# Expert loop of a hybrid layer: the down product runs one block later, weights arrive in halves, one Silu table load

## The reference

```python
def hier_moe(h, ...):                 # 32 experts, each token goes to 2
    ...
    padded = ((counts + MOE_BLOCK - 1) // MOE_BLOCK) * MOE_BLOCK   # MOE_BLOCK = 128
    ...
    def expert_block(args):
        xb, e = args                  # 128 rows of one expert
        hid = jax.nn.silu(xb @ w_gate[e]) * (xb @ w_up[e])
        return hid @ w_down[e]
    ...
```

## Time and profile before

| | |
|---|---|
| median of 3 runs | 2628.35 us (2627.71 to 2632.11) |
| span of the profiled execution | 2631.2 us |
| PE busy | 2182.8 us, 83% |
| DVE busy | 1414.4 us, 54% |
| ACT busy | 1110.2 us, 42% |
| DMA moved | 458.84 MB, mean 174 GB/s |

### The profile page before, as it was taken

One profiled execution on the slowest core, in us unless ns is written; L12 is line 12 of the kernel. 1 busy time (PEld: TensorE's weight loads), 2 busy tenths in 40 slices (PEclk: granted clock), 3 DMA queues, 4 the chain that ended last, 5 costly groups with the idle time before them and its releaser, 6 DMA issues. The chain is left out here.

```text
span 2631.2 us, 29505 instructions
## 1 busy us (share of the span) xinstructions
PE 2182.8 (83%) x9771; PEld 1642.8 (62%) x9772; DVE 1414.4 (54%) x2372; ACT 1110.2 (42%) x1586; POOL 310.3 (12%) x380
## 2 busy tenths in 40 slices
PE   4999999868969687785999219999999999999950
PEld 4764444357447676675888107777777777777740
DVE  4832581044358567584444527466647847354548
ACT  6101111013227566574222017566648847454432
POOL 0002331025020110000000220000000000000022
PEclk9999999979869899898999559999999999999985
DMA  7023433173651431502443057477668967445649
GB/s 220 34 78 136 168 136 116 51 263 128 260 142 46 100 71 43 112 1 71 140 140 125 17 208 296 197 273 311 250 244 308 368 248 300 186 187 203 252 169 377
DMA packets 129203, 458.84 MB, mean 174 GB/s; under 512 B 26192, under 2 KB 42720, under 8 KB 114784
## 3 DMA queue, kind: packets, MB, share of 16 engines
q1 hardware_dynamic: 98512, 345.28, 37.6%
q0 software_dynamic: 19952, 69.51, 7.1%
q10 hardware_dynamic: 10656, 43.00, 4.0%
HBM read 342.09 MB, written 115.65 MB: 174 GB/s over the span
## 5 line engine op out<-in xcount | busy, mean ns | idle before, releaser
L1532 DVE TENSOR_TENSOR w_gate_lo<-w_gate_raw,w_gate_hi 128x2048 fp32r<-128x2048 f32 x64 | 146.3, 2287 | 180.0 <-ACT w_gate_hi L1487 180.0
L895 DVE CUSTOM_DVE_ANT_0 scores<-c_bank,alibi 128x512 f32<-128x512 f32 (+3 forms) x320 | 175.4, 607 | 109.1 <-PE c_bank L993 108.9
L488 PE MATMUL a_bank<-w_in_chunk,hT 128*128 128x512 f32 x512 | 222.1, 596 | 0.7 <-ACT hT L266 0.7
L488 PE MATMUL a_bank<-hT,w_in_chunk 128*128 128x512 f32 x512 | 220.6, 593 | 0.0
L300 ACT ACTIVATE proj_out<-a_bank 128x512 f32<-128x512 f32 x64 | 38.2, 597 | 398.1 <-PE a_bank L488 387.8
L488 PEld LDWEIGHTS a_bank<-w_in_chunk,hT 128*128 128x128 f32 x512 | 128.8, 252 | 92.6 <-issue 62.8
L1007 PE MATMUL c_bank<-v_head,map_T 128*128 128x128 f32 x1088 | 152.0, 288 | 41.6 <-ACT map_T L951 41.6
L1575 PE MATMUL m_bank<-w_gate_hi,rows_T_hi 128*128 128x512 f32 x392 | 155.0, 395 | 24.1 <-DVE rows_T_lo L1536 24.1
L1613 PE MATMUL m_bank<-w_down_hi,hidden_T_hi 128*128 128x512 f32 x392 | 161.2, 411 | 16.5 <-ACT hidden_T_hi L1509 16.5
L488 PEld LDWEIGHTS a_bank<-hT,w_in_chunk 128*128 128x128 f32 x512 | 97.1, 190 | 120.8 <-issue 120.7
L1007 PEld LDWEIGHTS c_bank<-v_head,map_T 128*128 128x128 f32 x1088 | 135.9, 198 | 57.2 <-ACT map_T L951 57.2
(11 more groups left out here) (370 smaller groups left out, 4429.1 us busy)
## 6 DMA issues: line engine op xcount, KB each, us to landing
w_gate_raw<-in_w_gate_dram SPq DMA_DIRECT2D x32, 2048.0 KB
w_up_raw<-in_w_up_dram SPq DMA_DIRECT2D x32, 2048.0 KB
w_down_raw<-in_w_down_dram SPq DMA_DIRECT2D x32, 2048.0 KB
rows_d<-rows_out ACTq DMA_DIRECT2D x50, 512.0 KB, 10.5
rows_d<-zero_rows POOLq DMA_DIRECT2D x34, 512.0 KB
x_tile<-in_x_dram SPq DMA_DIRECT2D x16, 512.0 KB
w_in_chunk<-in_w_in_dram POOLq DMA_DIRECT2D x4, 2048.0 KB, 19.1
qT_d<-xn_tile SPq DMA_DIRECT2D x32, 256.0 KB
```

Source lines behind the costliest of these rows:

```text
L488: last = pe.matmul(bank[4 + n % PB][:], lhsT, rhs, start=kt == 0, stop=kt == KT - 1)
L895: dve.tensor_tensor_reduce(S[:, s, m, c * BANK:c * BANK + w], bank[n % 4][:, 0:w], bias[:, h % 2, x0:x0 + w], 1.0, -BIG, ALU.add, ALU.max, ...
L1532: dve.tensor_tensor(wlo[w][:, s], raw[w][:, s], whi[w][:, s], ALU.subtract).then_inc(lo_done[w], 1)
```

## The change

The down product of a block is issued one block later: TensorE's loop body is now gate product of block j + 1, hidden transposes of j, up product of j + 1, all eight row transposes of j + 2, down product of j. The first gate and up products stand ahead of the loop, the last block's hidden transposes and down product behind it, and the loop has one turn less (`META_LATER`, one more step in `route`). Each weight is loaded in two halves with a semaphore each, and each half waits for its own half of high and low part only. ACT makes both halves of the output. ACT and DVE get new orders, and split the first rows ahead of the first weights. ACT names the Silu table once ahead of its work.

```diff
+META_LATER = NBLK + NE + 2
+META = NBLK + NE + 3
...
+                step(dve.tensor_scalar(bf[:, META_LATER:META], pend[:, NE - 1:NE], -1.0, None, ALU.add))
...
-        w_in = [sem(f"w_{n}_in") for n in ("gate", "up", "down")]
+        w_in = [[sem(f"w_{n}_in{i}") for i in range(2)] for n in ("gate", "up", "down")]
...
+            later = lambda eng: eng.value_load(meta[0:1, META_LATER:META_LATER + 1], min_val=MIN_BLK - 1, max_val=NBLK - 2)
...
-                        sp.wait_ge(hi_done[w], 2 * o + 2)
-                        sp.wait_ge(lo_done[w], 2 * o + 2)
-                        sp.dma_start(raw[w][:], a[name][0, bass.ds(e, 1)].rearrange("o (p k) n -> p (o k n)", k=k)).then_inc(w_in[w], 16)
+                        src = a[name][0, bass.ds(e, 1)].rearrange("o (p k) n -> p (o k n)", k=k)
+                        for i in range(2):
+                            sp.wait_ge(hi_done[w], 2 * o + 1 + i)
+                            sp.wait_ge(lo_done[w], 2 * o + 1 + i)
+                            sp.dma_start(raw[w][:, halves[i]], src[:, halves[i]]).then_inc(w_in[w][i], 16)
...
+                def out_half(h, b):
+                    act.wait_ge(d_done, 2 * b + h + 1)
+                    if h == 0:
+                        act.wait_ge(out_st, 16 * b + 16)
+                    act.activation(out[:, h * BANK:(h + 1) * BANK], DN[h][:], ACT.Copy).then_inc(d_used, 1)
...
+                act.preload_act_table(ACT.Silu)
                 rows_hi(0, 1)
                 rows_hi(1, 2)
+                for w in range(3):
+                    split_hi(w, 0, 0)
+                    split_hi(w, 0, 1)
+                first, second = place(act, 0), place(act, 1)
+                act.wait_ge(g_done, 1)
+                act.activation(sil[:], G[:], ACT.Silu).then_inc(silu_done, 1)
+                with where_below(nc, act, first, second):
+                    split_hi(0, second, 0)
+                    split_hi(0, second, 1)
+                rows_hi(0, 3)
+                rows_hi(1, 4)
+                with where_below(nc, act, first, second):
+                    act.wait_ge(u_done, 1)
+                    split_hi(1, second, 0)
+                    split_hi(1, second, 1)
+                with act.Fori(0, later(act)) as j:
+                    before, now, order = place(act, j), place(act, j + 1), place(act, j + 2)
+                    hidden_hi(j + 1)
+                    act.wait_ge(g_done, j + 2)
+                    act.wait_ge(hid_done, j + 1)
                     act.activation(sil[:], G[:], ACT.Silu).then_inc(silu_done, 1)
                     with where_below(nc, act, now, order):
+                        split_hi(0, order, 0)
+                        split_hi(0, order, 1)
+                    rows_hi(0, 2 * j + 5)
+                    rows_hi(1, 2 * j + 6)
                     with where_below(nc, act, now, order):
+                        act.wait_ge(u_done, j + 2)
+                        split_hi(1, order, 0)
+                    out_half(0, j)
                     with where_below(nc, act, now, order):
+                        split_hi(1, order, 1)
+                    out_half(1, j)
+                    store(j)
+                    with where_below(nc, act, before, now):
+                        split_hi(2, now, 0)
+                        split_hi(2, now, 1)
+                end = later(act)
+                hidden_hi(end + 1)
+                out_half(0, end)
+                out_half(1, end)
+                store(end)
...
+                with dve.Fori(0, later(dve)) as j:
+                    before, now, order = place(dve, j), place(dve, j + 1), place(dve, j + 2)
+                    hidden_lo(j + 2)
                     with where_below(nc, dve, now, order):
+                        split_lo(0, order, 0)
+                        split_lo(0, order, 1)
+                    hidden(j + 1)
+                    rows_lo(0, 2 * j + 5)
+                    rows_lo(1, 2 * j + 6)
                     with where_below(nc, dve, now, order):
+                        split_lo(1, order, 0)
+                        split_lo(1, order, 1)
+                    with where_below(nc, dve, before, now):
+                        split_lo(2, now, 0)
+                        split_lo(2, now, 1)
+                end = later(dve)
+                hidden_lo(end + 2)
...
+                with pe.Fori(0, later(pe)) as j:
+                    before, order = place(pe, j), place(pe, j + 1)
+                    pe.wait_ge(xh_done, 2 * j + 4)
+                    pe.wait_ge(xl_done, 2 * j + 4)
+                    pe.wait_ge(silu_done, j + 1)
+                    pe.wait_ge(hi_done[0], 2 * order + 4)
+                    pe.wait_ge(lo_done[0], 2 * order + 4)
+                    product(G, 0, g_done)
+                    hidden_T(j)
+                    pe.wait_ge(hi_done[1], 2 * order + 4)
+                    pe.wait_ge(lo_done[1], 2 * order + 4)
+                    product(U, 1, u_done)
+                    pe.wait_ge(x_in, 16 * j + 48)
+                    rows_T(0)
+                    rows_T(1)
+                    down(j, before)
+                end = later(pe)
+                hidden_T(end)
+                down(end, place(pe, end))
```

More of the change, by code:

```diff
@@ L1391, in _ @@
                 step(dve.tensor_copy(bf[:, META_BLOCKS:META_BLOCKS + 1], pend[:, NE - 1:NE]))
-                step(dve.tensor_copy(bf[:, META_EXPERTS:META], order[:, NE - 1:NE]))
+                step(dve.tensor_copy(bf[:, META_EXPERTS:META_EXPERTS + 1], order[:, NE - 1:NE]))
+                step(dve.tensor_scalar(bf[:, META_LATER:META], pend[:, NE - 1:NE], -1.0, None, ALU.add))
                 step(dve.tensor_scalar(df[:, 0], order[:, NE - 1:NE], -1.0, None, ALU.add))
@@ L1483, in _, with split_hi @@
             def _(act):
[L1484 to L1487, removed]
+                def split_hi(w, order, i):
+                    act.wait_ge(w_in[w][i], 16 * order + 16)
+                    act.activation(whi[w][:, halves[i]], raw[w][:, halves[i]], ACT.Copy).then_inc(hi_done[w], 1)
                 def rows_hi(h, want):
@@ L1491, in rows_hi, with hidden_hi @@
                     act.activation(xh[:, 4 * h:4 * h + 4], XT[h][:].rearrange("p (k t) -> p k t", k=4), ACT.Copy).then_inc(xh_done, 1)
-                for w in range(3):
-                    split_hi(w, 0)
+                def hidden_hi(want):
+                    act.wait_ge(hT_psum, want)
+                    act.activation(hh[:], HT[:].rearrange("p (k t) -> p k t", k=FT), ACT.Copy).then_inc(hh_done, 1)
+                def out_half(h, b):
[3 more added lines that the diff above has]
+                    act.activation(out[:, h * BANK:(h + 1) * BANK], DN[h][:], ACT.Copy).then_inc(d_used, 1)
@@ L1495, in _, with store @@
+                def store(b):
+                    act.wait_ge(d_used, 2 * b + 4)
+                    act.dma_start(d["rows"][bass.ds(b, 1)].rearrange("o p n -> p (o n)"), out[:]).then_inc(out_st, 16)
+                act.preload_act_table(ACT.Silu)
                 rows_hi(0, 1)
                 rows_hi(1, 2)
[L1497 to L1503, removed]
+                for w in range(3):
+                    split_hi(w, 0, 0)
+                    split_hi(w, 0, 1)
@@ L1527, in _, with split_lo @@
             def _(dve):
[L1528 to L1532, removed]
+                def split_lo(w, order, i):
+                    dve.wait_ge(hi_done[w], 2 * order + 3 + i)
+                    dve.tensor_tensor(wlo[w][:, halves[i]], raw[w][:, halves[i]], whi[w][:, halves[i]],
+                                      ALU.subtract).then_inc(lo_done[w], 1)
                 def rows_lo(h, want):
@@ L1537, in rows_lo, with hidden, hidden_lo @@
                                       ALU.subtract).then_inc(xl_done, 1)
-                for w in range(3):
-                    split_lo(w, 3)
+                def hidden(b):
+                    dve.wait_ge(u_done, b + 1)
+                    dve.wait_ge(silu_done, b + 1)
+                    dve.tensor_tensor(hid[:], sil[:], U[:], ALU.mult).then_inc(hid_done, 1)
+                def hidden_lo(want):
+                    dve.wait_ge(hh_done, want)
+                    dve.tensor_tensor(hl[:], HT[:].rearrange("p (k t) -> p k t", k=FT), hh[:], ALU.subtract).then_inc(hl_done, 1)
@@ new lines, in _ @@
+                for w in range(3):
+                    split_lo(w, 0, 0)
+                    split_lo(w, 0, 1)
+                first, second = place(dve, 0), place(dve, 1)
+                with where_below(nc, dve, first, second):
+                    split_lo(0, second, 0)
+                    split_lo(0, second, 1)
+                hidden(0)
+                rows_lo(0, 3)
+                rows_lo(1, 4)
+                with where_below(nc, dve, first, second):
+                    split_lo(1, second, 0)
+                    split_lo(1, second, 1)
@@ L1578, in product, with hidden_T @@
                     last.then_inc(done, 1)
[L1580 to L1590, removed]
```

(5 more changed lines are left out.)

61 lines of the change are left out of this document (20 added, 41 removed).

## The result

The changed kernel takes 2648.02 us (median of 4 runs, 2646.46 to 2651.34) where the kernel before takes 2630.23 (4 runs): 1.0064 times as long, with a 95% interval of 1.005 to 1.0078. That is slower by 0.6%, small but clear of the spread. The forecast was 2552 us. The profiled execution has a span of 2643.9 us.

What follows compares the result with a forecast made beforehand. TensorE was taken to bound the expert loop, busy 920.8 of 962 us. Saving 76.0 us (start some 14, late arrivals 6, the rest 1.2 to 1.3 a block) gave span 2555.2, less 2.9 to the median: 2552 us, range 2545 to 2572.

Steps and rivals of the forecast that it cites:

- Down product one block later: TensorE's expert loop: both gaps in a block go, period 18.2 us without a wait, 1.2 to 1.3 less a block.
- Halves: SP's weight loads: six issues instead of three cost nothing; gate's 14.0 us window ends late arrivals, 6 us.
- DMA bytes: DMA engines in changing blocks: 7.34 MB need 17.6 to 18.8 us; cost taken as 0, bounds 0 and 19 us.
- Rival A: DMA becomes the bound where expert changes follow each other: 2565 us, or 2571 with all 31 changes; chance 0.13.
- Rival C: SP's queue serves half loads one at a time: slower, 2654 us, or 2705 by the documented fixed cost; chance 0.03.
- The fixed cost of each half: SP's loads: about 2.0 us a DMA, 26 us an expert if served serially; the prediction held the trace against that.
- Table loads: ACT's table loads ahead of gate high and silu in the loop: worth 0 us now and 0 after.
- Start: Ahead of the loop: rows split first and gate in halves bring the first gate product about 15 us earlier.
- End: Behind the loop: last hidden transposes to down product 1.58 us in the open, then 5.87, 7.5 in all.
- The store's room: Output store in the loop: 15.4 us to land before the next output copy instead of 14.1; median landing 10.5.
- Rival D: The loop stays what it was, hidden or rows waiting on something missed; only 14 us gained, 2614 us; chance 0.03.
- The sign that the prediction set down for rival A: TensorE in the runs of expert changes: waiting for gate's or the rows' low part would show the forecast wrong.

Runs made afterwards that it cites:

- e10_order_again: e1_order measured once more, unchanged, in five later rounds: 2563.42 us (2561.17 to 2564.86).
- e9_halves: e4_start with each weight loaded in two halves with a semaphore each, down product left where it was: 2609.52 us.
- e1_order: The changed kernel with SP issuing gate and up loads of the expert after next ahead of the next one's down load: 2562.35 us, 0.9745 of the kernel before.
- e2_order_whole: e1_order with one load of 2 MB a weight, waiting for both halves, instead of two half loads: 2563.29 us.
- e5_no_preload: e1_order without the line that names the Silu table ahead of the loop: 2563.80 us.
- e4_start: The kernel before with only the first block's rows split ahead of the first weights: 2618.76 us, 0.9968 of before.
- e6_last_same: e1_order with the last block computed by the previous expert's weights, the last expert's neither loaded nor split (wrong rows): 2558.11 us.
- e8_more_bytes: e1_order with 1.05 MB more an expert on SP's queue, a copy of half the gate weights: 2572.69 us.

## Why the prediction was wrong

By its steps:

- *Down product one block later*: right, in the words as in the size. 18.16 us an iteration (18.2), no wait in it, both gaps gone. e10_order_again is 46 us under e9_halves, which has the start and the halves. From the first gate product to the next phase it is 912.6 (e1_order, 1557.50 to 2470.10) against 961.9 us (e9_halves), 49.3 less. The gate products of e9_halves lie 19.37 us apart without a change and 19.52 with one, so 48 iterations save some 63 us. Of that the longer end takes some 8 (below), and the second gate product some 6, its wait of 4.2 and the clock behind it.
- *Halves*: **this is the step that failed**, the cost of nothing for SP and the window of 14 us. It said "Six DMA issues of about 0.34 us an expert on SP instead of three: SP idles, no cost", and "the first half is free at 11.5 and wanted at 7.3 + 18.2, 14.0 us later". Free it was; but free for a load that SP had not come to. I listed what is queued behind what on ACT and DVE, and not on SP, though the down split had been moved a block against the gate split, and SP's program had not been. By the prediction's own numbers down's low part is done at 25.0 and gate is wanted at 25.5, so the window was 0.5 us and not 14. e1_order against the changed kernel prices that at 86 us: nine waits of 65.0 us in all and the clock that falls in each (about 2 us a time, since the matmuls behind it start 0.43 apart at first, as in the earlier trace rows). The forecast was lost there: with the order mended the time is 2562, inside the range of 2545 to 2572.
- *DMA bytes*: right that they fit (share 1.00 to 1.01 in the runs, 401 to 408 GB/s, no wait), and 0 was the right value between the bounds. Rival A would not have saved the forecast. Rival C had the sign right with a mechanism that isn't there; e2_order_whole and e1_order are 1 us apart. The reading against it was a little too plain: by 5.0 us for 2.10 MB at 418 GB/s the second and third load of the earlier trace rows, 6.2 and 4.9 behind the one before, took 1.1 us more than their bytes.
- *The fixed cost of each half*: the prediction takes its 2.0 us from the Trainium skill's page DMA: Bandwidth & Descriptors, Anatomy of one DMA. That section gives them for DMAs issued from GpSimd, and these are SP's; no run takes a load of SP alone. They do not add up over queued loads. By the runs, 7.34 MB are 18.0 us at 408 GB/s, and the run of seven keeps its 18.16 us a block with six half loads as with three whole ones. Six costs of 2.0 us one behind the other would be 12 us more, which that block has no room for.
- *Table loads*: 0, as said, and they left the loop, but not by the line that names the table (e5_no_preload).
- *Start*: 15 us forecast for halves and order together; 15.7 seen, from the first row transposes to the first product (1545.25 to 1555.62, 10.4 us, against 26.1). The 18.3 us between the starts as they stand hold 2.6 of an earlier stage. e4_start and e9_halves bring 11 and 21 by the medians, the latter with the late arrivals.
- *End*: mis-sized. 1.58 + 5.87 us left out that the last step is a change of expert, though the prediction has down's low part done only at 25.0, 6.8 us after the last iteration's end. Down waits 7.51 us for it and then starts at the low clock: 15.8 us from the last hidden transposes to the end (2449.76 to 2465.59) instead of 7.5. What goes when the weights no longer hold it up is 4 us by e6_last_same's medians, 6.5 by its trace. The start, the iterations and what follows were each put about 1 us too long, so that the span of e1_order, 2559.8, lies 4.6 over the 2555.2 of the sum. The other 5.7 us of its distance to 2552 are no term of the loop: the prediction took 2.9 off to come from the span of one run to the median of others, while in e1_order the median lies 2.5 above the profiled span.
- *The store's room*: by the prediction's own times 14.8 us and not 15.4 (18.8 to 33.6); with landings of 10.5 it bears on nothing.

Rival D priced a loop that stays what it was; none of the rivals had a load queued behind another. The sign that the prediction set down for rival A, TensorE waiting for gate low in the runs, is what came. That sign could not tell bytes from order. The DMA share could: 0.67 over the run of seven, where A needs it near 1.

## What to carry to other kernels

A consumer that is moved an iteration later moves the time at which its buffer is free, and so the place that its load must have in the program of the queue that issues it. Before such a change write down, for one iteration, when each buffer becomes free, and issue the loads in that order. A window of 14 us between free and wanted is worth nothing if the issuing engine waits for another buffer. The trace tells it in one view: the issuing queue's own waits, and the distance from the last read of a buffer to the issue of its next load.

## What the runs showed of the hardware

- With weights, row gathers and stores together the DMA engines held 401 to 408 GB/s at a share of 1.00 to 1.01 over 18 us stretches of e1_order. That is what the loop asks for (7.34 MB in 18.16 us are 404), so a share of 1.00 does not yet say that time is lost: e8_more_bytes has 413 to 422 at the same share. The 391 that I scaled up from a share of 0.94 was too low.
- A stall ahead of a gate product costs more than its length: after 5.4 us of idle time the next matmul takes 0.77 instead of 0.39, and the gate product behind one of the nine waits takes 7.0 to 8.2 us up to the hidden transposes instead of 5.6. The granted clock is 0.50, the lower of its two levels (1.2 GHz), from 2011.10 to 2013.60, behind 8.09 us of idle time; in the stretch from 2005 to 2105 it is 0.86 for the changed kernel against 1.00 for e1_order. 85.0 us of difference between the two (997.6 against 912.6 from the first gate product to the next phase) stand against 65.0 us of waits.
- A switch of ACT's table costs 1.28 us here and nothing beside it: the load of the earlier trace rows at 2055.53 begins where the activation before it ends, and the next one starts 0.02 us behind its end:

```profile
2053.60 1.92 ACT L1487 ACTIVATE w_gate_hi<-w_gate_raw 128x2048 fp32r<-128x2048 f32 x1
...
2056.83 0.60 ACT L1504 ACTIVATE silu<-m_bank 128x512 f32<-128x512 f32 x1
```
